# A hybrid-mixer block on one core: the output product of the second mixer summed over four outputs at a time

## What is computed

```python
def hybrid_mixer(x, mix_norm, w_in, conv_w, conv_b, dt_bias, a_log, d_skip, ssd_norm, rel_bias, w_out):
    bsz, seqlen, _ = x.shape
    h = rms_norm(x, mix_norm)
    proj = h @ w_in
    ...
    y = ssd_chunked(xs, dt, a, bm, cm, d_skip).reshape(bsz, seqlen, SSD_INNER)
    y = rms_norm(y * jax.nn.silu(z.astype(jnp.float32)), ssd_norm).astype(x.dtype)
    att = chunked_rel_attention(q, k, v, rel_bias).astype(x.dtype)
    return jnp.concatenate([y, att], axis=-1) @ w_out

...
        x = x + hybrid_mixer(x, mix_norm[i], w_in[i], conv_w[i], conv_b[i], dt_bias[i], a_log[i],
                             d_skip[i], ssd_norm[i], rel_bias[i], w_out[i])
        x = x + 0.5 * swiglu(rms_norm(x, ffn2_norm[i]), ffn2_w_gate[i], ffn2_w_up[i], ffn2_w_down[i])
    return rms_norm(x, final_norm)
```

## Time and profile before

| | |
|---|---|
| time of three runs | 1980.04, 1982.24, 1983.16 us; median 1982.24 |
| span of the profiled execution | 1980.1 us |
| its own device time | not given beside the span; the span is 2.1 under the median |
| TensorE busy | 1929.7 us, 97% of the span |
| VectorE, ScalarE, GpSimd busy | 48%, 46%, 40% |
| early blocks to end of the output product | about 1519.5 to 1601.9 us |
| chain that ended last | 91% TensorE, 4% VectorE, 2% ScalarE |

### The profile page before, as it was taken

The page is one execution under the profiler, slowest core; times in us unless marked ns, Lnnn a source line. Parts: engine busy times, 40 slices in busy tenths (PEclk is TensorE's granted clock), DMA queues, the critical chain, the costliest instruction groups (busy, mean ns, idle before and its releaser), DMA issues.

```text
span 1980.1 us, 25387 instructions
## 1 busy us (share of the span) xinstructions
PE 1929.7 (97%) x8744; PEld 1571.3 (79%) x8744; DVE 945.3 (48%) x1135; ACT 917.5 (46%) x1220; POOL 786.2 (40%) x357
## 2 busy tenths in 40 slices
PE   6999999999999999999999999999999999999998
PEld 5777777777788888888888888787776788888886
DVE  6666666676434343223344422356677643434312
ACT  5577777776555553223222222467676332222222
POOL 0233333334344444443444444443332434444443
PEclk9999999999999999999999999999999999999999
DMA  7333333323222222222222233222221222222232
GB/s 302 116 102 123 126 127 127 127 100 126 83 96 95 95 95 96 96 96 96 95 95 95 95 107 106 85 75 82 77 74 65 75 85 97 99 99 97 96 106 74
DMA packets 54617, 203.17 MB, mean 103 GB/s; under 512 B 6064, under 2 KB 6192, under 8 KB 53296
## 3 DMA queue, kind: packets, MB, share of 16 engines
q1 hardware_dynamic: 54576, 202.62, 30.3%
HBM read 200.50 MB, written 2.10 MB: 102 GB/s over the span
## 4 chain that ended last, share of the span: by engine, by line
PE 91%; DVE 4%; ACT 2%; issue 2%; POOL 1%; DMA 0%; POOLq 0%; ACTq 0%; DVEq 0%
PE bank L614 26%; PE bank L615 26%; PE bank L619 25%; PE bank L764 1%; PE bank L974 1%; PE bank L976 1%; PE bank L975 1%; PE bank L772 1%; PE bank L1007 1%; PE bank L736 1%; DVE TG L1589 1%; POOL WL L509 1%; PE bank L1036 1%; DVE MIX L1589 1%; PE bank L825 1%
## 5 line engine op out<-in xcount | busy, mean ns | idle before, releaser
L509 POOL TENSOR_TENSOR WL<-ring,WH 128x1024 fp32r<-128x1024 f32 (+1 forms) x318 | 763.0, 2400 | 1144.7 <-ACT WH L1124 1144.7
L1124 ACT ACTIVATE WH<-ring 128x1024 fp32r<-128x1024 f32 (+2 forms) x326 | 339.0, 1042 | 845.5 <-PE bank L619 769.1
L614 PE MATMUL bank<-HH,WL 128*128 128x512 f32 x1744 | 690.1, 396 | 7.4 <-POOL WL L509 4.1
L615 PE MATMUL bank<-HH,WH 128*128 128x512 f32 x1744 | 684.5, 392 | 0.0
L619 PE MATMUL bank<-HL,WH 128*128 128x512 f32 x1744 | 431.6, 389 | 0.3 <-DVE HL L1589 0.3
L614 PEld LDWEIGHTS bank<-HH,WL 128*128 128x128 f32 x1744 | 331.1, 190 | 77.1 <-POOL WL L509 5.0
L615 PEld LDWEIGHTS bank<-HH,WH 128*128 128x128 f32 x1744 | 331.1, 190 | 68.0
L619 PEld LDWEIGHTS bank<-HL,WH 128*128 128x128 f32 x1744 | 327.4, 188 | 69.1 <-DVE HL L1589 1.3
L614 PE MATMUL bank<-FH,WL 128*128 128x512 f32 x544 | 211.7, 389 | 0.0
L615 PE MATMUL bank<-FH,WH 128*128 128x512 f32 x544 | 211.7, 389 | 0.0
L619 PE MATMUL bank<-FL,WH 128*128 128x512 f32 x544 | 135.0, 389 | 0.0
(11 more groups left out here) (331 smaller groups left out, 2083.9 us busy)
## 6 DMA issues: line engine op xcount, KB each, us to landing
ring<-in_stream SPq DMA_DIRECT2D x355, 512.0 KB, 3.3
ARENA<-in_ada SPq DMA_DIRECT2D x8, 1024.0 KB, 13.2
ring<-in_stream SPq DMA_DIRECT2D x8, 448.0 KB, 11.1
XT<-in_xt SPq DMA_DIRECT2D x2, 1024.0 KB, 6.6
result<-XT SPq DMA_DIRECT2D x3, 512.0 KB, 2.6
result<-XT SPq DMA_DIRECT2D x2, 256.0 KB, 2.1
vec<-in_vec SPq DMA_DIRECT2D x1, 220.0 KB, 2.7
```

The source lines that it names most:

```text
L509: nc.gpsimd.tensor_tensor(WL[:, slot, 0:cols], ring[:, u % RING, 0:cols], WH[:, slot, 0:cols].bitcast(F32), ALU.subtract).then_inc(w_low, 1)
L614: mm(out_ap, part(WL, base, loc, k), xh(k), start=(start and k == 0), stop=False)
L615: mm(out_ap, part(WH, base, loc, k), xh(k), start=False, stop=False)
L1124: A(WH[:, split_at(base, loc)[1], 0:cols], ring[:, u % RING, 0:cols], ACT.Copy).then_inc(w_high, 1)
```

## The change

`OUT2` gets another order. Outputs 0 to 3 are now summed together: first 12 blocks (k = 0 to 2 for each of the four, output by output, `OUT2_STARTED`), then for each k from 3 to 11 the four blocks of that input (`out2_across`), and only then outputs 4 to 7, one after the other, as before. All eight outputs have a bank of their own (`OUT2_BANK`).

- The 12 started blocks lie in the last pair: six where they were, three (output 2) behind a wait for the last skip (`y_skip`), which reads bank 2, then `token_sums`, one block, `turn(1)`, `spread`, one block, `values`, one block. `values` of the last pair goes to bank 0, since bank 7 holds output 3.
- `out2_across(k)` waits for the high half of input k, does the eight products with it, waits for the low half and does the four with that.
- ScalarE makes the high weights of unit 2 before `turned(1)`, and GpSimd splits that unit ahead of its four low halves of y, where it stood behind them. ScalarE makes the high halves of y in two groups of four, with the weights of unit 3 between.
- VectorE takes the four residuals of outputs 0 to 3 first, then their four low halves, then their squares. ScalarE's four high halves follow by pairs the weight copies n = 5 and n = 6 (`OUT2_HIGH`); those of outputs 4 to 7 follow n = 7, 8, 10 and 11.
- `silu_up(4)` waits for output 4's residual only (8 * 4 + 5) ahead of its first gate product in bank 0, and for all eight behind the first up product.

```diff
-OUT2_EARLY = 6
-OUT2 = [(_m, _k) for _k in range(3) for _m in range(2)]
-OUT2 = sorted(OUT2) + [(0, _k) for _k in range(3, 12)] + [(1, _k) for _k in range(3, 12)]
-OUT2 += [(_m, _k) for _m in range(2, KD) for _k in range(12)]
-OUT2_BANK = [1, 3, 0, 2]
+OUT2_STARTED = 12
+OUT2 = [(_m, _k) for _m in range(4) for _k in range(3)]
+OUT2 += [(_m, _k) for _k in range(3, 12) for _m in range(4)]
+OUT2 += [(_m, _k) for _m in range(4, KD) for _k in range(12)]
+OUT2_BANK = [1, 3, 2, 7, 0, 4, 5, 6]
+OUT2_LAST = [OUT2.index((_m, 11)) for _m in range(KD)]
+OUT2_ENDS_UNIT = [_b % BLOCKS == BLOCKS - 1 for _b in OUT2_LAST]
+OUT2_HIGH = {5: (0, 1), 6: (2, 3), 7: (4,), 8: (5,), 10: (6,), 11: (7,)}
...
-                if loc == 10:
+                if loc == 11:
                     lows(40, YH, states_low)
...
+            def out2_across(k):
+                blocks = range(OUT2_STARTED + 4 * (k - 3), OUT2_STARTED + 4 * (k - 2))
+                if k < 4:
+                    pe.wait_ge(r["o_high"], k + 1)
+                else:
+                    pe.wait_ge(h_high, 40 + k - 4 + 1)
+                for b in blocks:
+                    to, wh, wl, xh, xl = out2_parts(b)
+                    mm(to, wl, xh, start=False, stop=False)
+                    mm(to, wh, xh, start=False, stop=False)
+                if k < 4:
+                    pe.wait_ge(r["o_low"], k + 2)
+                else:
+                    low_wait(40, k - 4)
+                for b in blocks:
+                    m = OUT2[b][0]
+                    wh = part(WH, U_OUT2, b // BLOCKS, b % BLOCKS)
+                    xl = tile_of(ML, k) if k < 4 else states_low(k - 4)
+                    out2_done(b, mm(bank[OUT2_BANK[m]][:, :], wh, xl, start=False, stop=(k == 11)))
...
                     pe.wait_ge(r["z_silu"], 8)
-                    out2(0, OUT2_EARLY)
+                    out2(0, 6)
+                    pe.wait_ge(r["y_skip"], 10)
+                    out2(6, 9)
                     pe.wait_ge(r["yss_done"], 8)
                     token_sums(4).then_inc(r["yms"], 1)
+                    out2(9, 10)
                     turn(1)
                     pe.wait_ge(r["yrc"], 1)
                     spread(4).then_inc(r["yrs"], 1)
+                    out2(10, 11)
+                    values(0)
+                    out2(11, 12)
...
-            out2(OUT2_EARLY, len(OUT2))
+            for k in range(3, 12):
+                out2_across(k)
+            out2(OUT2.index((4, 0)), len(OUT2))
...
+                    act.wait_ge(unit_done, U_OUT2 + 1)
+                    weight_high(U_OUT2, 2)
                     turned(1)
...
-            high_of_mix(r["ynorm"], 0, YH)
-            for n in range(12):
+            high_of_states(0, 4)
+            for n in range(1, 12):
                 act.wait_ge(unit_done, U_OUT2 + n + 1)
                 weight_high(U_OUT2, n + 2)
-                for m in range(KD):
-                    if (12 * m + 11) // BLOCKS == n:
-                        high_of_x(4, m, "ffn2_norm_2")
+                if n == 1:
+                    high_of_states(4, KD)
+                for m in OUT2_HIGH.get(n, ()):
+                    high_of_x(4, m, "ffn2_norm_2")
...
+            for m in range(4):
+                out2_residual(m)
+            for m in range(4):
+                low_of_x(m, 48, "ffn2_norm_2")
+            for m in range(4):
+                out2_square(m)
+            for m in range(4, KD):
+                out2_residual(m)
+                dve.wait_ge(res_done, 8 * 4 + m + 1)
+                low_of_x(m, 48, "ffn2_norm_2")
+                out2_square(m)
```

More of the change, by code:

```diff
@@ L958, in _, with out2_parts, out2_done @@
             pe.wait_ge(r["tr_evac"], 2)
+            def out2_parts(b):
+                unit = b // BLOCKS
+                if b % BLOCKS == 0:
+                    split_wait(U_OUT2, unit)
+                m, k = OUT2[b]
+                xh, xl = (tile_of(MH, k), tile_of(ML, k)) if k < 4 else (tile_of(YH, k - 4), states_low(k - 4))
+                return bank[OUT2_BANK[m]][:, :], part(WH, U_OUT2, unit, b % BLOCKS), part(WL, U_OUT2, unit, b % BLOCKS), xh, xl
+            def out2_done(b, last):
+                if b % BLOCKS == BLOCKS - 1:
+                    last.then_inc(unit_done, 1)
+                elif OUT2[b][1] == 11:
+                    last.then_inc(r["yms"], 1)
             def out2(first, end):
@@ L962, in out2 @@
                     m, k = OUT2[b]
[L963 to L966, removed]
                     if k < 4:
                         pe.wait_ge(r["o_low"], k + 2)
[L969 to L973, removed]
+                    to, wh, wl, xh, xl = out2_parts(b)
                     mm(to, wl, xh, start=(k == 0), stop=False)
                     mm(to, wh, xh, start=False, stop=False)
[L976 to L980, removed]
+                    out2_done(b, mm(to, wh, xl, start=False, stop=(k == 11)))
+            def out2_across(k):
[5 more added lines that the diff above has]
+                for b in blocks:
+                    to, wh, wl, xh, xl = out2_parts(b)
+                    mm(to, wl, xh, start=False, stop=False)
[9 more added lines that the diff above has]
+                    out2_done(b, mm(bank[OUT2_BANK[m]][:, :], wh, xl, start=False, stop=(k == 11)))
             def pair(t, is_last):
@@ L1038, in turn, with values @@
                     last.then_inc(r["t_mm"], 1)
-                def values():
+                def values(b):
                     pe.wait_ge(r["t_evac"], 6 * t + 9)
@@ L1096, in pair @@
                     proj(4, 10)
-                values()
+                    values(7)
             with pe.Fori(0, 3) as t:
@@ L1140, in high, with high_of_states @@
                         A(tile_of(HH, k), tile_of(MIX, k), ACT.Identity, bias=MOD[:, col + k:col + k + 1]).then_inc(h_high, 1)
-            def high_of_mix(done, before, H=HH):
-                for k in range(KD):
-                    act.wait_ge(done, before + k + 1)
-                    A(tile_of(H, k), tile_of(MIX, k), ACT.Copy).then_inc(h_high, 1)
+            def high_of_states(first, end):
+                for k in range(first, end):
+                    act.wait_ge(r["ynorm"], k + 1)
+                    A(tile_of(YH, k), tile_of(MIX, k), ACT.Copy).then_inc(h_high, 1)
             def high_of_x(n, k, gain, i=0):
@@ L1557, in pair @@
                 act.wait_ge(r["pv_mm"], 2 * t + 2)
[L1558 removed]
+                A(tile_of(MH, t), bank[0 if is_last else 7][:, :], ACT.Copy).then_inc(r["o_high"], 1)
             with act.Fori(0, 3) as t:
@@ L2102, in _, with out2_residual, out2_square @@
             clear_ss(CLEAR[4])
[L2103 to L2105 removed]
+            def out2_residual(m):
+                if OUT2_ENDS_UNIT[m]:
+                    dve.wait_ge(unit_done, U_OUT2 + OUT2_LAST[m] // BLOCKS + 1)
                 else:
[L2107 removed]
+                    dve.wait_ge(r["yms"], 1 + OUT2_ENDS_UNIT[:m + 1].count(False))
                 x = tile_of(XT, m)
[L2109 removed]
+                STT(x, bank[OUT2_BANK[m]][:, :], one[:, :], x, ALU.mult, ALU.add).then_inc(res_done, 1)
+            def out2_square(m):
                 dve.wait_ge(res_done, 8 * 4 + m + 1)
[L2111 removed]
+                x = tile_of(XT, m)
                 if m % 4 == 3:
                     TT(CG[:, m // 4, :], x, x, ALU.mult).then_inc(sq_done, 1)
[L2114 removed]
+                    return
                 TT(SQ[:, :], x, x, ALU.mult).then_inc(sq_done, 1)
```

16 lines of the change are left out of this document (4 added, 12 removed).

## The result

| | before | after |
|---|---|---|
| median of the runs on one chip, us | 1981.49 (1980.04 to 1983.16, 4 runs) | 1970.47 (1970.23 to 1976.53, 4 runs) |
| ratio, 95% interval | | 0.9947 (0.9932 to 0.9962) |
| span of the profiled execution, us | 1980.1 | 1974.7 (its own time 1976.53) |
| TensorE busy, us | 1929.7 | 1929.9 |
| all runs of this study, mean us | 1982.4 (88 runs) | 1971.9 (20 runs) |

The change makes the kernel 10.5 us, 0.53%, faster. The forecast was 1974.1 with a range of 1970.7 to 1977.7: the 20 runs of the changed kernel, unaltered in four comparisons, had medians of 1970.47, 1972.04, 1971.29 and 1971.5.

The account below looks back on a forecast made before the run. TensorE, busy 1929.7 of 1980.1 us, was taken to bound the kernel. A hole-free gain of 9.85 less 1.7 for VectorE's heap gave 8.15, off the median 1982.24: 1974.1 us, range 1970.7 to 1977.7.

Parts of the forecast that it names:

- (1): Last pair: three blocks wait for bank 2, run 1524.52 to 1526.70, when squares are ready; 0.8 us of hole stays.
- (2): Token sums and second head's turn: turn late by 0.1 us, at full clock, to 1529.35; spread to 1530.15.
- (3): Last pair's values start at 1530.95, now 1532.07; MH is ready at 1534.05, with block 11 in that gap.
- (4): Inputs 3 to 5 over four outputs: low halves hide behind products; waits of 1.4, 1.1, 1.6 us go; to 1542.3.
- (6): Last 72 blocks at 0.686 us take 49.4, ending 1592.0 if nothing waits, 9.85 us against 1601.85.
- the heap: VectorE's piled work for four outputs ending together makes weights of units 10 and 11 late by 1.2 and 0.5 us.
- Step 5: Unit 3's split on GpSimd, behind four low halves, ends at 1542.45; TensorE waits some 0.3 us, to 1542.6.
- the zero charged for changing banks: Summing over four outputs changes bank every product or second product; seven earlier products took 0.226 us each, so nothing charged.
- (a): Rival: VectorE's piled work after input 11 costs nothing; gain 9.3 to 9.85 us, 1972.4 to 1972.9; chance 0.2.
- The sum: Net gain from the early blocks to the next projection: 9.85 less 1.7 gives 8.15 us.
- rival (b): Clock falls all the same behind the one-column token sums; gain 6.6 us, 1975.6; chance 0.15.
- rival (c): Half-clock stretches elsewhere, as at 1617 to 1619.5, lost or found by earlier arrival: 1.5 us either way; no own chance.

Follow-up runs that it names:

- act_order: Changed kernel with ScalarE's high halves of outputs 4 and 5 each one weight copy later; 1972.4 us, ratio 0.9945.
- before_busy: Kernel before the change with nine unread products in the 2.81 us hole ahead of the token sums; 1979.17 us, ratio 0.9985.
- across_busy: Kernel before with only the input-by-input summing, six started blocks moved behind the values, and nine unread products in the hole; 1976.26 us, ratio 0.997.
- before_again: Kernel before the change, unaltered, run again; 1980.99 us, ratio 0.9995.
- across_only: Kernel before with only the input-by-input summing: six blocks in the last pair, the other six behind the values; 1978.33 us, ratio 0.998.
- fill_only: Kernel before with only the 12 started blocks in the last pair, then outputs summed one after another; 1976.25 us, ratio 0.9973.
- squares_late: Changed kernel with VectorE's squares of outputs 2 and 3 behind residuals 4 and 5, those of 4 to 6 behind residual 6; 1977.98 us, ratio 0.9981.
- after_again: Changed kernel, unaltered, run a second time; ratio 0.9951 to the kernel before.
- after_b: Changed kernel, unaltered, run a third time; ratio 0.9946 to the kernel before.
- act_order_b: Second run of the changed kernel with ScalarE's high halves of outputs 4 and 5 one weight copy later; ratio 0.9962.
- act_order_c: Third run of the changed kernel with ScalarE's high halves of outputs 4 and 5 one weight copy later; ratio 0.9952.

## Why the prediction was right, and where not, point by point

Times from the start of the first started block, the prediction's by its steps (before's 1519.48 taken off) against after's profile:

| step | predicted | after |
|---|---|---|
| seventh block starts | 5.04 | 5.04 |
| token sums (1) | 7.22 | 7.22 |
| turn of the second head (2) | 8.8 | 8.91 |
| values (3) | 11.5 | 11.68 |
| input 3 (4) | 14.6 | 14.79 |
| next projection, hole-free (6) | 72.5 | 72.75 (act_order) |
| with the heap | 74.2 | 73.90 |

**Steps 1 to 4** held to 0.2 us: of the hole a wait for the skip's bank stays, 0.64 by its bracket and 0.80 from start to start, as put in step 1; the turn runs at full clock, and beyond that no started block, weight copy or bank waits. No low half of y is waited for. before_busy shows that step 2's clock was the hole's doing.

**Step 5** put 0.3 before unit 3's products; input 6 came about 0.2 behind its even spacing, so the right size, with no bracket in the timeline; unit 3's split took 2.85 and ended at 1546.55, the product began at 1546.70. across_busy shows what the early end of unit 0 and the early copy of unit 2 are worth: without them there is a hole of 1.06.

**Step 6**, 0.686 for a block, held, and so did the zero charged for changing banks.

**The heap** had the right mechanism, place and cause, and was mis-sized: 1.7 predicted (1.2 and 0.5), 1.15 measured. The residual of output 4 was put at T+17.75 and came at 1580.57, T+17.3 with T = 1563.3, the end of input 11, which ScalarE's copy of 1563.38 waited for; the copy of unit 10 came at T+18.7, not 19.2. The line that failed is "split 9 to 14.85, the next ends 15.4": I let a square hold GpSimd there, but VectorE's and GpSimd's timelines show that the split began 0.2 ahead of the square and only the square lost:

```profile
1574.98 0.69 DVE L2156 TENSOR_TENSOR SQ<-XT 128x512 f32<-128x512 f32 x1
1575.70 2.77 DVE L2158 TENSOR_TENSOR SS<-SS,SQ 128x512 f32<-128x512 f32 x1
...
1580.57 0.75 DVE L1627 SCALAR_TENSOR_TENSOR XT<-bank,one,XT 128x512 f32<-128x512 f32 x1
```

```profile
1575.50 2.42 POOL L512 TENSOR_TENSOR WL<-ring,WH 128x1024 fp32r<-128x1024 f32 x1 [3.09 <-ACT WH L1159]
1583.11 2.67 POOL L512 TENSOR_TENSOR WL<-ring,WH 128x1024 fp32r<-128x1024 f32 x1 [5.19 <-ACT WH L1159]
```

The square begun at 1575.70 ends with the split of 1575.50 and 0.55 behind; the split of 1583.11, for unit 10, is the one that was held, 2.67 against 2.42. The held square ends at T+15.2 and not 15.4, so this line is about 0.2 of the 0.5; the rest is the three squares and the residual behind it, 2.85 us where 3.1 had been put. On TensorE the first product of unit 10 starts 0.70 later than even spacing and that of unit 11 0.15, where 1.2 and 0.5 had been put, and each pause adds the 0.11 of its first product.

The Trainium skill's page "SBUF — State Buffer", section "SBUF: two separate sides", says that a VectorE operation with two SBUF inputs and a GpSimd operation that reads SBUF shut each other out, whoever is first. The trace agrees: squares are held by splits (2.77) and a split by a square (2.67). The rival that squares go free, which gave (a), is out.

**The sum** was 8.15 for the stretch and 8.47 was found. Two errors offset each other in part: the heap is 0.55 cheaper, and the hole-free gain is 82.37 - 72.75 = 9.62, not 9.85. In that gain the clock is 1.1 by before_busy, where rival (b) had put it at 1.5; before_busy's longer wait for the turned weights, 0.31 more, is the most of that difference.

**What the sum left out** is the rest: 10.5 in the whole time against 8.5 in the stretch. The prediction took the clock elsewhere as 1.5 either way, with no expected value (rival (c)). The runs show a gain: the mean clock rises by 0.0026, 3.3 us by the slope, of which 1.1 to 2.1 lie in the stretch. The four profiles of after have no fall at the next norm, those of before have 3.4 us at 1616.5 and 6.8 at 1614.0. So the medians lie 2.1 to 3.6 us below the forecast, and three of the four are inside the range only because (c) was in it: the mechanism in the stretch was right, but the gain outside it was not forecast, and that it stayed inside the range is in part luck. Of the rivals, (a) gave nearly the right time (1972.4 to 1972.9) for a wrong reason: the heap did cost 1.15.

## What to carry over

Before a short wait on the engine that sets the end is written off as a few microseconds, look at the granted clock behind it: here 2.8 us of standing cost 1.1 to 2.1 more in the work after it, and work moved into the hole earned both. Not every hole of that length has this price (see below), so look at several profiles. When several outputs end together, follow each engine's fixed order past that point: the wait appears where a copy that could run stands behind one that can't, two engines from the heap. Measure a stretch that both programs share, and take the clock's state into account before a whole-time difference of 2 us is believed: a real 1.13 us in the stretch didn't show in 18 runs.

## What the runs showed of the hardware

**A hole, and what it costs the clock.** Behind 2.81 us without work and eight one-column products the granted clock was 0.50, the 1.2 GHz level, for 3.4 us (before), 6.8 (before_again, across_only); with nine products in the hole it stayed 1.00. Holes of 1.60 (fill_only) and 1.07 (across_only) brought no fall right behind them; 3.33 (squares_late) did. The low stretch may outlast the sparse work: in before_again the clock is back at 1.00 only at 1532. But the length of a hole doesn't settle it. In the wait near 95 us, with products of 512 columns on both sides, 3.39 us (after_again), 3.20 (fill_only) and 3.73 (squares_late) left the clock at 1.00, and 3.29 (after_b) was followed by 0.50. TensorE's timeline and window, first of after_again, then of after_b:

```profile
98.59 0.50 PE L617 MATMUL bank<-HH,WL 128*128 128x512 f32 x1 [3.39 <-POOL WL L512]
```

```profile
98.00:102.00 4.00, 3.41 (x15) 1.00 0.53 188
```

```profile
96.99 0.50 PE L617 MATMUL bank<-HH,WL 128*128 128x512 f32 x1 [3.29 <-POOL WL L512]
```

```profile
98.00:101.00 3.00, 3.00 (x9) 0.52 0.51 175
```

**Falls under full load.** At the next norm, with TensorE busy 6.80 of 6.80 us, the clock fell in some kernels' profiles and not in others':

```profile
1614.00:1620.80 6.80, 6.80 (x19) 0.51 0.26 77
```

That is before_again; after is at 1.00 there in four profiles of four, before_busy too. Over the runs of before, the clock goes with about 60% of the spread between runs (correlation -0.77, slope 1.28 us per 0.001). Over those of after, 1969 to 1977 us, it is about 20% (correlation -0.47); the wait near 95 us, 3.29 to 5.06 in its profiles, is another part, and the rest is open.

The Trainium skill's page "TensorE: Matmul & The Clock Gate", Part 1, says the gate runs free of the kernel's start. Falls of one and the same program do come and go from profile to profile: one near 910 us is in three of the four profiles of after and not in the fourth, which agrees. The 907 against 1617 of rival (c) does not bear on this: both lie in one execution, and show two places rather than one place met twice. What sets the fall at the norm stays open. With the early hole filled it is missing in the profiles of after, before_busy and across_busy, but there, for 3.4 us, in those of fill_only (1612.1) and of act_order_b and act_order_c; with the hole open it was there in all three (before, before_again, across_only).
